# Up projections with one 512-column product for the high weights, a VectorE sum of two banks, and the gate product on GpSimd

## The chip, the cores and the metric

The kernel runs on one core of a Trainium2 chip. The core has TensorE (matmuls into PSUM, eight banks of 128 partitions x 512 float32), VectorE, ScalarE and GpSimd (elementwise work), and SyncE, which here only issues loads. The engines run side by side and are ordered by semaphores alone. The metric is the device time of one execution, in microseconds; lower is better.

## The reference

Four layers run over a residual stream x of 256 tokens x 1024 channels. Each layer has a mixer (sparse attention in layers 0 and 3, RWKV-7 in layer 1, S5 in layer 2) and then a conv-gated MLP, which is all that the change touches:

```
def conv_ffn(h, w_up, conv_w, conv_b, w_down):      # D = 1024, F = 2816
    u = h @ w_up                                     # (256, 1024) @ (1024, 5632)
    u = lax.conv_general_dilated(u, conv_w[:, None, :], ... feature_group_count=u.shape[-1]) + conv_b
    gate, val = jnp.split(u, 2, axis=-1)             # causal convolution over 3 tokens, per channel
    return (jax.nn.silu(gate) * val) @ w_down        # (256, 2816) @ (2816, 1024)

for i in range(DEPTH):                               # DEPTH = 4
    ...                                              # mixer
    h = rms_norm(x, norm_ffn[i])
    x = x + conv_ffn(h, ffn_w_up[i], ffn_conv_w[i], ffn_conv_b[i], ffn_w_down[i])
```

## The kernel before

Everything is kept transposed: channels on partitions, the T = 256 tokens along the free axis. A float32 product is made of three matmuls on rounded parts. A weight block is split into high (rounded on ScalarE, line 397) and low (what is left, line 405); the activations likewise, into x_high and x_low. `product` (line 420) issues high x high, high x low and low x high, 256 columns each, into the same 256 columns of PSUM (lines 422 to 424).

A *tile* is 1024 x 256 weights (1 MB), loaded by SyncE into a ring of three slots (line 697). It has two blocks of 128 output channels, b = 0 and 1. ScalarE rounds both blocks; VectorE computes the low part of block 0 and GpSimd that of block 1 (`rest_of_weights`, line 399). There are two buffers of split weights, so tile k + 2 is split while tile k + 1 is in use, and a block can be rounded once TensorE has done with the same block two tiles before (`ahead`, line 407; `wait_half`, line 359). SyncE reloads a slot once both low parts are made (`wait_slot`, line 680).

**The up stage** of a layer has 22 tiles in 11 pairs: tile 2j holds gate channels, 2j + 1 the value channels for them. Pairs 0 to 2 are written out, pairs 3 to 8 run in a hardware loop of two rounds, pairs 9 and 10 are written out again (`over_up_tiles`, line 755). A tile has 8 chunks x 2 blocks = 16 products. Before, both blocks of a tile go to the two halves of one PSUM bank, bank i mod 6, so six tiles fit. Pair 0 uses `early` activations, not yet scaled by the norm, and its banks are scaled afterwards (line 908). Tile 2 takes its chunks as VectorE finishes x_low (line 557).

What follows a tile: ScalarE forms tap 2 of the convolution from the bank (line 856), VectorE adds taps 1 and 0 (line 937, four instructions a tile, counting `taps_done` 2 per tile). For a pair ScalarE takes the silu of the gate half (line 862), VectorE multiplies gate and value (line 946, into `gated`), ScalarE rounds this to inner_high (line 841), and GpSimd computes inner_low (line 885, counting `inner_ready`).

**The down stage** follows on TensorE: four outputs m, three weight tiles g each. For m < 3 it already uses a pair: high weights times inner_high and inner_low as one 512-column matmul (line 824), low weights times inner_high (line 826), and VectorE adds the two halves of the bank (lines 662 and 664). m = 3 uses `product`. Output m and block b go to bank DOWN_BANKS[m] + b, for m = 0 banks 4 and 5.

Which bank TensorE may overwrite is planned ahead: `plan.fill` counts the fills of each bank, `freed` names the semaphore value at which a fill has been read, and `wait_free` (line 328) waits for that of the fill before. Layer 1 also prepares layer 2's mixer: `s5_turn_a` (line 2683) behind pair 9 and `s5_turn_c` (line 2690) behind pair 10 transpose parameters into banks 6 and 7. In layers 0 and 3 the last mixer outputs alternate between banks 0 and 1; line 642 adds them to x.

## Time and profile before

| | us |
|---|---|
| median of 3 runs | 1431.87 (1431.63 to 1433.32) |
| the profiled execution | 1431.35 |
| its span, first to last instruction | 1429.6 |

The profile is that of one execution. Engine names in it: PE is TensorE's matmuls, PEld its weight loads, DVE is VectorE, ACT ScalarE, POOL GpSimd, SP SyncE. L405 is line 405 of the kernel. Matmuls overlap, and their ends are modelled: distances between starts tell the pace. In layer 0 tile 0 starts at 154.61 us, tile 3 at 173.62, the down stage at 283.16. PEclk is the granted clock of TensorE, 1.00 being 2.4 GHz and 0.50 being 1.2 GHz.

### The profile page before, as it was taken

What the parts mean: (1) busy time and instruction counts of PE and PEld (TensorE: products, weight loads), DVE (VectorE), ACT (ScalarE), POOL (GpSimd) and SP (SyncE); (2) the same over time, 40 slices, a digit from 0 to 9 for tenths busy, and PEclk for the clock granted to TensorE, in tenths of its full rate; (3) what the DMA queues carried; (4) which work ended last, traced back from release to release, by engine and by line L of the source; (5) the groups of instructions that cost most, each with busy time, mean ns of one, the idle gap of its engine ahead of it and who ended that gap; (6) DMA issues with size and microseconds to landing.
All of it is one profiled execution on the core that took longest, in us unless ns stands there. A gap on an engine that the chain in (4) does not pass through costs nothing.

```text
span 1429.6 us, 33183 instructions
## 1 busy us (share of the span) xinstructions
PE 1378.5 (96%) x13785; PEld 1302.5 (91%) x13785; DVE 1011.5 (71%) x1604; ACT 804.3 (56%) x1331; POOL 659.0 (46%) x370
## 2 busy tenths in 40 slices
PE   8999999999999887999999889999999999999998
PEld 8999999989888777999988779999989998999988
DVE  6675887834595556897789966888746685888841
ACT  5576666644751453666554445656645577676642
POOL 4343365552003630495557945365544332365552
PEclk9999999999999999999999999999999999999999
DMA  6542455553534011475554024465554543455553
GB/s 200 183 133 96 159 196 185 184 189 119 148 124 142 4 34 32 148 224 190 169 180 153 2 62 152 148 203 178 183 197 128 179 146 119 148 179 188 186 172 102
DMA packets 208168, 209.60 MB, mean 147 GB/s; under 512 B 7954, under 2 KB 207170, under 8 KB 208034
## 3 DMA queue, kind: packets, MB, share of 16 engines
q1 hardware_dynamic: 207168, 206.21, 44.8%
q0 software_dynamic: 800, 1.46, 0.6%
q8 instruction: 100, 1.64, 0.5%
q14 instruction: 34, 0.28, 0.1%
q10 hardware_dynamic: 66, 0.02, 0.0%
HBM read 206.62 MB, written 1.05 MB: 145 GB/s over the span
## 4 chain that ended last, share of the span: by engine, by line
PE 82%; DVE 11%; ACT 4%; issue 2%; POOL 1%; DMA 0%; ACTq 0%; DVEq 0%; POOLq 0%
PE psum L422 17%; PE psum L424 17%; PE psum L423 17%; PE psum L824 9%; PE psum L605 6%; PE psum L826 4%; DVE x_low L557 2%; DVE work L2958 1%; ACT w_high L397 1%; DVE work L542 1%; PE psum L1800 1%; PE psum L1817 1%; DVE w_low L405 1%; PE psum L1089 1%; PE psum L1100 1%
## 5 line engine op out<-in xcount | busy, mean ns | idle before, releaser
L405 POOL TENSOR_TENSOR w_low<-ring,w_high 128x1024 fp32r<-128x1024 f32 (+1 forms) x185 | 460.4, 2489 | 611.4 <-ACT w_high L397 589.5
L422 PE MATMUL psum<-x_high,w_high 128*128 128x256 f32 x1728 | 491.2, 284 | 5.0 <-DVE x_low L2375 2.8
L397 ACT ACTIVATE w_high<-ring 128x1024 fp32r<-128x1024 f32 (+1 forms) x368 | 376.4, 1036 | 212.2 <-PE psum L424 119.5
L424 PE MATMUL psum<-x_high,w_low 128*128 128x256 f32 x1728 | 488.9, 283 | 0.0
L423 PE MATMUL psum<-x_low,w_high 128*128 128x256 f32 x1728 | 488.9, 283 | 0.0
L405 DVE TENSOR_TENSOR w_low<-ring,w_high 128x1024 fp32r<-128x1024 f32 x183 | 299.4, 1637 | 169.6 <-ACT w_high L397 168.2
L422 PEld LDWEIGHTS psum<-x_high,w_high 128*128 128x128 f32 x1728 | 331.6, 192 | 7.4 <-issue 3.4
L423 PEld LDWEIGHTS psum<-x_low,w_high 128*128 128x128 f32 x1728 | 331.7, 192 | 0.0
L424 PEld LDWEIGHTS psum<-x_high,w_low 128*128 128x128 f32 x1728 | 331.6, 192 | 0.0
L824 PE MATMUL psum<-inner,w_high 128*128 128x512 f32 x528 | 186.8, 399 | 0.0
L937 DVE SCALAR_TENSOR_TENSOR work<-psum,par,work 128x255 f32<-128x255 f32 (+1 forms) x352 | 144.6, 472 | 45.8 <-ACT work L856 45.7
L856 ACT ACTIVATE work<-psum,par 128x256 f32<-128x256 f32 x176 | 89.3, 561 | 131.3 <-PE psum L424 131.3
L826 PE MATMUL psum<-inner,w_low 128*128 128x256 f32 x528 | 148.3, 281 | 0.0
L824 PEld LDWEIGHTS psum<-inner,w_high 128*128 128x128 f32 x528 | 99.2, 188 | 24.6
L826 PEld LDWEIGHTS psum<-inner,w_low 128*128 128x128 f32 x528 | 99.8, 189 | 0.0
L946 DVE TENSOR_TENSOR work<-work 128x512 f32<-128x512 f32 x44 | 80.9, 1839 | 7.4 <-DVE work L937 5.5
L605 PE MATMUL psum<-work,ring 128*128 128x256 f32 x384 | 84.4, 379 | 0.9 <-issue 0.9
L605 PEld LDWEIGHTS psum<-work,ring 128*128 128x128 f32 x384 | 72.8, 190 | 13.0 <-issue 3.4
L422 PE MATMUL psum<-w_high,x_high 128*128 128x256 f32 x256 | 75.1, 293 | 0.0
L885 POOL TENSOR_TENSOR inner<-work,inner 128x512 f32 (+1 forms) x44 | 74.8, 1703 | 0.0
L424 PE MATMUL psum<-w_high,x_low 128*128 128x256 f32 x256 | 72.4, 283 | 0.0
L423 PE MATMUL psum<-w_low,x_high 128*128 128x256 f32 x256 | 72.4, 283 | 0.0
(353 smaller groups left out, 2212.0 us busy)
## 6 DMA issues: line engine op xcount, KB each, us to landing
ring<-in_ffn_w_up_dram SPq DMA_DIRECT2D x88, 1024.0 KB, 5.1
ring<-in_ffn_w_down_dram SPq DMA_DIRECT2D x32, 1024.0 KB, 5.2
ring<-in_dsa_w_in_dram SPq DMA_DIRECT2D x28, 1024.0 KB, 5.3
ring<-in_ffn_w_down_dram SPq DMA_DIRECT2D x16, 768.0 KB, 4.4
ring<-in_rwkv_w_rkv_dram SPq DMA_DIRECT2D x12, 1024.0 KB, 5.1
ring<-in_dsa_w_out_dram SPq DMA_DIRECT2D x8, 1024.0 KB, 5.4
ring<-in_s_w_glu_dram SPq DMA_DIRECT2D x8, 1024.0 KB, 5.4
ring<-in_rwkv_w_out_dram SPq DMA_DIRECT2D x4, 1024.0 KB, 5.1
```

The source lines that it names most:

```text
L397: act.activation(high, raw, ACT.Copy).then_inc(sem("w_rounded", b), 1)
L405: eng.tensor_tensor(low, raw, high.bitcast(F32), ALU.subtract).then_inc(sem("w_split", b), 1)
L422: pe.matmul(out_, lhs[0], rhs[0], start=start, stop=False, skip_group_check=True)
L423: pe.matmul(out_, lhs[0], rhs[1], start=False, stop=False, skip_group_check=True)
L424: return pe.matmul(out_, lhs[1], rhs[0], start=False, stop=stop, skip_group_check=True)
L605: mm = pe.matmul(out_, parts[b][:, k, b * P:(b + 1) * P], x[:, k, :], start=start, stop=stop, skip_group_check=True)
L824: pe.matmul(banks[bank][:, :], high[:, k, :], inner[:, :, c, :], start=first, stop=False, skip_group_check=True)
L826: mm = pe.matmul(banks[bank][:, 0:T], low[:, k, :], inner_high[:, c, :], start=False, stop=last, skip_group_check=True)
L856: act.activation(conv[:, j % 3, h, b, :], bank_of(key)[:, b * T:(b + 1) * T], ACT.Identity, bias=col("ffn_conv_b", c + L * 2 * FC, r), sca ...
L885: pool.tensor_tensor(inner_low[:, at(2 * j, r), :], gated[:, j % 3], inner_high[:, at(2 * j, r), :].bitcast(F32), ALU.subtract).then_inc(s ...
L937: dve.scalar_tensor_tensor(out=row, in0=bank[:, b * T:(b + 1) * T - lag], scalar=col("ffn_conv_w", c + (L * 3 + tap) * 2 * FC, r), in1=row ...
L946: dve.tensor_tensor(gated[:, j % 3], conv[:, j % 3, 0], conv[:, j % 3, 1], ALU.mult).then_inc(sem("gated_done"), 1)
```

## The change

From tile 2 on, the three matmuls of a product become two: high weights times x_high and x_low side by side (`x_both`, the same memory as x_high and x_low), 512 columns, which fill a whole bank, and low weights times x_high into its first half. So each block of a tile gets a bank of its own: tile i uses banks 2 (i mod 3) and the next, and three tiles fit instead of six. Tiles 0 and 1 keep the three matmuls, but use two banks too.

When a tile's two banks are full, VectorE adds their halves (`tensor_reduce` over 2 x 256 x 2 elements) into a sum bank: 6 or 7 in turn, 2 or 3 for tiles 20 and 21. Taps read the sum bank. ScalarE rounds both blocks of the tile after next before tap 2, which waits for the sum (`halves_added`). The product of gate and value moves from VectorE to GpSimd. `freed` says when a tile's banks may be filled again: after its sum for tiles 2 to 18, after its own taps for tiles 0 and 1, and after all taps of the layer (2 * FC = 44) for tiles 19 to 21. `s5_turn_a` waits for the taps of tile 18, as bank 6 is in use now.

```diff
-        simple([(L, "up", i) for i in range(2 * FC // 2)], split=True)
+        for i in range(FC):
+            plan.weights((L, "up", i), split=True)
+            for b in range(2):
+                plan.fill((L, "up", i, b), 2 * (i % (NBANK // 2)) + b)
+            plan.used[(L, "up", i)] = ("bank_full", plan.bank[(L, "up", i, 1)])
...
-                freed[(L, "up", 2 * j)] = (("taps_done", L), 4 * j + 2)
-                freed[(L, "up", 2 * j + 1)] = (("taps_done", L), 4 * j + 4)
+                for b in range(2):
+                    for h in range(2):
+                        i = 2 * j + h
+                        freed[(L, "up", i, b)] = ((("halves_added", L), i + 1) if 1 < i < FC - 3 else
+                                                  (("taps_done", L), 2 * i + 2 if i < 2 else 2 * FC))
...
+                        if j == 0:
+                            mm = product(pe, banks[bank][:, 0:T], (high, low), (early[0][:, c, :], early[1][:, c, :]),
+                                         c == 0, c == DC - 1)
+                        else:
+                            pe.matmul(banks[bank][:, :], high, x_both[:, :, c, :], start=c == 0, stop=False,
+                                      skip_group_check=True)
+                            mm = pe.matmul(banks[bank][:, 0:T], low, x_high[:, c, :], start=False, stop=c == DC - 1,
+                                           skip_group_check=True)
+                        if c == DC - 1:
+                            mm.then_inc(sem("bank_full", bank), 1)
...
+        def half_sums(key):
+            i = key[2]
+            if i < 2:
+                first = plan.bank[(*key, 0)][0]
+                return psum[:, first:first + 2, 0:T]
+            return banks[6 + i % 2 if i < FC - 2 else 2 + i % 2].rearrange("p (b t) -> p b t", b=2)
+        def halves(key):
+            first = plan.bank[(*key, 0)][0]
+            return psum[:, first:first + 2, :].rearrange("p b (a t) -> p b t a", a=2)
...
                     if j:
-                        ahead(round_weights, act, key, 0, r=r)
-                        wait_full(act, key, r)
-                    else:
-                        act.wait_ge(sem("scaled"), h + 1 + since("scaled", L))
+                        ahead(round_weights, act, key, r=r)
+                    act.wait_ge(sem("halves_added"), r * ROUND + (2 * j + h + 1 + since("halves_added", L)))
...
+            def gate_times_value(j, r):
+                pool.wait_ge(sem("silu_done"), r * PJ + (j + 1 + since("silu_done", L)))
+                pool.wait_ge(sem("taps_done"), r * (4 * PJ) + (4 * j + 4 + since("taps_done", L)))
+                if j >= 3:
+                    pool.wait_ge(sem("inner_ready"), r * PJ + (j - 2 + since("inner_ready", L)))
+                pool.tensor_tensor(gated[:, j % 3], conv[:, j % 3, 0], conv[:, j % 3, 1],
+                                   ALU.mult).then_inc(sem("gated_done"), 1)
             def pair(j, r):
+                ahead(rest_of_weights, pool, (L, "up", 2 * j), 1, r=r)
+                if j:
+                    gate_times_value(j - 1, r)
+                ahead(rest_of_weights, pool, (L, "up", 2 * j + 1), 1, r=r)
                 if j:
                     rest_of_inner(j - 1, r)
...
                 for h in range(2):
+                    key = (L, "up", 2 * j + h)
+                    sums = half_sums(key)
                     if j:
-                        ahead(rest_of_weights, dve, (L, "up", 2 * j + h), 0, r=r)
+                        both_full(key, r)
+                        dve.tensor_reduce(out=sums, in_=halves(key), op=ALU.add, axis=AX_X).then_inc(sem("halves_added"), 1)
+                        ahead(rest_of_weights, dve, key, 0, r=r)
...
-        def s5_turn_a(pe):
+        def s5_turn_a(pe, L):
             pe.wait_ge(sem("s5_in", 0), 16 * S5_DMAS[0])
+            pe.wait_ge(sem("taps_done"), 2 * (FC - 4) + 2 + since("taps_done", L - 1))
```

## Rows read from the trace of the kernel before

**Rows 1.** The page: busy time (us), share of the span and instructions per engine.

```profile
PE 1378.5 (96%) x13785; PEld 1302.5 (91%) x13785; DVE 1011.5 (71%) x1604; ACT 804.3 (56%) x1331; POOL 659.0 (46%) x370
```

**Rows 2.** The page: the chain that ended last, shares of the span by engine and by line.

```profile
PE 82%; DVE 11%; ACT 4%; issue 2%; POOL 1%; DMA 0%; ACTq 0%; DVEq 0%; POOLq 0%
PE psum L422 17%; PE psum L424 17%; PE psum L423 17%; PE psum L824 9%; PE psum L605 6%; PE psum L826 4%; DVE x_low L557 2%; DVE work L2958 1%; ACT w_high L397 1%; DVE work L542 1%; PE psum L1800 1%; PE psum L1817 1%; DVE w_low L405 1%; PE psum L1089 1%; PE psum L1100 1%
```

**Rows 3.** Busy time per stretch, layer 0's up stage and start of its down stage.

```profile
core 0: us, PE busy (x) PEld busy (x) DVE busy (x) ACT busy (x) POOL busy (x), PEclk, DMA share, GB/s
172.00:283.00 111.00, 110.71 (x923) 110.51 (x922) 92.03 (x116) 70.98 (x102) 65.51 (x29) 1.00 0.54 178
283.00:325.00 42.00, 42.00 (x240) 36.46 (x239) 16.66 (x18) 18.05 (x21) 21.38 (x10) 1.00 0.61 193
```

**Rows 4.** Timeline of PE: start us, duration us, engine, line, operation [idle before, releaser].

```profile
173.62 0.39 PE L422 MATMUL psum<-x_high,w_high 128*128 128x256 f32 x1 [0.29 <-DVE w_low L405]
...
283.16 0.40 PE L824 MATMUL psum<-inner,w_high 128*128 128x512 f32 x1
...
329.80 0.28 PE L422 MATMUL psum<-inner,w_high 128*128 128x256 f32 x1
```

**Rows 5.** Groups by form (count, busy us, mean ns, idle before); a timeline row; the page's load.

```profile
L2958 DVE TENSOR_TENSOR work<-b_sum,psum 128x1024 f32<-128x1024 f32 x4 | 4.9, 1221 | 0.1
...
791.10 2.34 DVE L2958 TENSOR_TENSOR work<-work,psum 128x1024 f32<-128x1024 f32 x2
...
L1348 DVE TENSOR_REDUCE work<-work 128x8 f32<-128x512 f32 x8 | 5.4, 680 | 0.0
L2146 POOL TENSOR_TENSOR work<-work,blocks 128x512 f32<-128x512 f32 x8 | 10.0, 1275 | 38.7 <-ACT work L2056 38.7
ring<-in_ffn_w_up_dram SPq DMA_DIRECT2D x88, 1024.0 KB, 5.1
```

**Rows 6.** Groups of instructions in the stretch 172 to 283 us.

```profile
L405 DVE TENSOR_TENSOR w_low<-ring,w_high 128x1024 fp32r<-128x1024 f32 x21 | 41.1, 1957 | 6.5 <-ACT w_high L397 6.5
L937 DVE SCALAR_TENSOR_TENSOR work<-psum,par,work 128x255 f32<-128x255 f32 (+1 forms) x84 | 34.5, 472 | 10.4 <-ACT work L856 10.4
```

**Rows 7.** Timelines of VectorE, GpSimd and ScalarE near layer 0's last up tiles.

```profile
274.64 2.23 DVE L946 TENSOR_TENSOR work<-work 128x512 f32<-128x512 f32 x1
276.79 2.31 DVE L405 TENSOR_TENSOR w_low<-ring,w_high 128x1024 fp32r<-128x1024 f32 x1
...
284.42 1.65 DVE L937 SCALAR_TENSOR_TENSOR work<-psum,par,work 128x255 f32<-128x255 f32 x4 [1.24 <-ACT work L856]
...
273.88 2.44 POOL L405 TENSOR_TENSOR w_low<-ring,w_high 128x1024 fp32r<-128x1024 f32 x1 [3.31 <-ACT w_high L397]
276.29 1.74 POOL L885 TENSOR_TENSOR inner<-work,inner 128x512 fp32r<-128x512 f32 x1
285.41 2.43 POOL L405 TENSOR_TENSOR w_low<-ring,w_high 128x1024 fp32r<-128x1024 f32 x1 [3.32 <-ACT w_high L397]
...
283.36 1.02 ACT L856 ACTIVATE work<-psum,par 128x256 f32<-128x256 f32 x2 [1.76 <-PE psum L424]
284.27 1.06 ACT L397 ACTIVATE w_high<-ring 128x1024 fp32r<-128x1024 f32 x1
```

**Rows 8.** Timeline of VectorE at layer 0's first up tiles.

```profile
172.35 1.21 DVE L405 TENSOR_TENSOR w_low<-ring,w_high 128x1024 fp32r<-128x1024 f32 x1
173.61 3.21 DVE L937 SCALAR_TENSOR_TENSOR work<-psum,par,work 128x255 f32<-128x255 f32 x8
```

**Rows 9.** Timelines of VectorE and PE around layer 0's tile 0.

```profile
154.81 0.69 DVE L642 TENSOR_TENSOR xT<-xT,psum 128x512 f32<-128x512 f32 x1 [0.92 <-PE psum L424]
...
154.61 0.28 PE L422 MATMUL psum<-early_high,w_high 128*128 128x256 f32 x1
157.84 1.10 PE L505 MATMUL psum<-work,mean_all 128*128 128x256 f32 x4 [0.19 <-DVE work L493]
```

**Rows 10.** Timeline of PE at the end of layer 1's up stage.

```profile
715.73 1.03 PE L2696 MATMUL psum<-ident,work 128*128 128x128 f32 x8
716.52 0.48 PE L824 MATMUL psum<-inner,w_high 128*128 128x512 f32 x1
```

**Rows 11.** Timeline of PE behind idle time, and the stretches around (columns as rows 3).

```profile
898.89 0.39 PE L422 MATMUL psum<-early_high,w_high 128*128 128x256 f32 x1 [1.91 <-DVE work L3068]
...
900.30 0.41 PE L422 MATMUL psum<-early_high,w_high 128*128 128x256 f32 x1
900.94 0.41 PE L422 MATMUL psum<-early_high,w_high 128*128 128x256 f32 x1
...
898.00:900.00 2.00, 1.11 (x8) 1.11 (x9) 1.53 (x3) 1.76 (x3) 0.00 (x0) 0.94 1.05 361
900.00:902.00 2.00, 2.00 (x11) 2.00 (x10) 1.54 (x3) 2.00 (x5) 0.00 (x0) 0.50 0.28 98
902.00:904.00 2.00, 2.00 (x11) 1.94 (x11) 1.23 (x1) 0.92 (x1) 1.00 (x1) 0.71 0.00 0
...
825.66 2.06 PE L2741 MATMUL psum<-work 128*64 128x32 f32 x64 [2.07 <-DVE psum L2999]
```

More of the change, by code:

```diff
@@ L54 @@
 NBANK = 6
+UP_FILLS = 2
 DOWN_BANKS = (4, 0, 2, 4)
@@ L128, in weights @@
             self.split_tiles.append(key)
-            if key[1:2] + key[3:] != ("down", 2):
+            if key[1] != "up" and key[1:2] + key[3:] != ("down", 2):
                 self.half[key] = len(self.half) + 1
@@ L783, in pair @@
                     if j >= PJ:
-                        name, value = freed[(L, "up", 2 * j + h - ROUND)]
+                        name, value = freed[(L, "up", 2 * j + h - NBANK // 2, 0)]
                         done, offset = signal(name)
-                        pe.wait_ge(done, r * (4 * PJ) + (value + offset))
+                        pe.wait_ge(done, r * ROUND + (value + offset))
                     else:
-                        wait_free(pe, key)
-                    bank = plan.bank[key][0]
+                        for b in range(2):
+                            wait_free(pe, (*key, b))
                     parts, first = {}, h == 0 and j < 2
-                    high, low = early if j == 0 else (x_high, x_low)
                     for c, b in chunks_and_blocks(DC, first):
@@ L797, in pair @@
                             parts[b] = split_weights(pe, key, b, r)
-                        mm = product(pe, banks[bank][:, b * T:(b + 1) * T], (parts[b][0][:, c, :], parts[b][1][:, c, :]),
-                                     (high[:, c, :], low[:, c, :]), c == 0 and (b == 0 or not first), c == DC - 1)
-                        half_done(key, mm, b == 0 and c == DC - 1)
-                    mm.then_inc(sem("bank_full", bank), 1)
+                        high, low, bank = parts[b][0][:, c, :], parts[b][1][:, c, :], plan.bank[(*key, b)][0]
+                        if j == 0:
[8 more added lines that the diff above has]
+                            mm.then_inc(sem("bank_full", bank), 1)
                 if before_s5(L) and j == UP_TILES // 2 - 2:
-                    s5_turn_a(pe)
+                    s5_turn_a(pe, L + 1)
                 if before_s5(L) and j == UP_TILES // 2 - 1:
@@ L896, in mlp_pool @@
             over_up_tiles(pool, pair)
+            gate_times_value(UP_TILES // 2 - 1, 0)
             rest_of_inner(UP_TILES // 2 - 1, 0)
@@ L937, in pair, with both_full @@
                             dve.scalar_tensor_tensor(
-                                out=row, in0=bank[:, b * T:(b + 1) * T - lag],
+                                out=row, in0=sums[:, b, 0:T - lag],
                                 scalar=col("ffn_conv_w", c + (L * 3 + tap) * 2 * FC, r),
                                 in1=row, op0=ALU.mult, op1=ALU.add).then_inc(done, 1)
-                dve.wait_ge(sem("silu_done"), r * PJ + (j + 1 + since("silu_done", L)))
-                dve.wait_ge(sem("taps_done"), r * (4 * PJ) + (4 * j + 4 + since("taps_done", L)))
-                if j >= 3:
-                    dve.wait_ge(sem("inner_ready"), r * PJ + (j - 2 + since("inner_ready", L)))
-                dve.tensor_tensor(gated[:, j % 3], conv[:, j % 3, 0], conv[:, j % 3, 1],
-                                  ALU.mult).then_inc(sem("gated_done"), 1)
+            def both_full(key, r):
+                for b in range(2):
+                    bank, n = plan.bank[(*key, b)]
+                    dve.wait_ge(sem("bank_full", bank), r * UP_FILLS + n)
             over_up_tiles(dve, pair)
```

27 lines of the change are left out of this document (14 added, 13 removed).

## The prediction

> **What bounds the kernel now.** I read the page's totals first: TensorE is busy 96% of the span, VectorE 71%, GpSimd 46% [rows 1]. The chain that ended last agrees: 82% of it is TensorE, led by the three product lines 422 to 424 [rows 2]. The busy time per stretch then shows how full the up stage of layer 0 is: from 172 to 283 us TensorE is busy 110.7 of 111 us, and in the down stage that follows 42.0 of 42 [rows 3]. So both stages run at the pitch of the matmuls, and any wait put on TensorE is paid in full. A matmul's printed duration (0.28 or 0.40 us) is not its price, because neighbours overlap; the start-to-start distance is.
>
> **What the pair saves.** The up stage issues triples of 256 columns. From the first matmul of tile 3 at 173.62 to the first of the down stage at 283.16 are 19 tiles of 16 triples: 109.54 / 304 = 0.3603 us each. The down stage already issues the pair that the change introduces (512 columns, then 256): from 283.16 to 329.80 are 132 pairs, 0.3533 us each [rows 4]. The 512-column matmul takes the time of the two it replaces, and only 0.007 us per triple is left. Tiles 3 to 21 save 304 x 0.0070 = 2.13 us per layer, 8.5 us in four. Tile 2 saves nothing: it follows x_low, which VectorE finishes late. A tile becomes 16 x 0.3533 = 5.65 us long.
>
> **What it costs in steady state.** Per tile VectorE loses half a gate product and gains a reduce over 1024 PSUM elements. The nearest rows are VectorE operations on 1024 elements with a PSUM operand, 1.22 us, or 1.13 start to start; TENSOR_REDUCE itself is seen only at 512 elements, 0.68 us as other operations of that size [rows 5]. I take 1.14; twice that is the upper end, as this reduce writes 512 results and reads across two banks.
>
> The real price is in how VectorE and GpSimd meet. The split of a weight block takes VectorE 1.21 us alone [rows 8], but 1.96 on average in the up stage, while its taps stay at 0.47 [rows 6]. The timeline shows why. The gate product asked at 274.64 while GpSimd's split ran 273.88 to 276.32, and ended at 276.87: 0.55 after. VectorE's split asked at 276.79 while GpSimd's L885 ran until 278.03, and ended at 279.10: 1.07 after [rows 7]. An operation of one with two SBUF inputs waits until the other's is done. The order is by who asks first, and a waiting VectorE gets its turn between two GpSimd operations: L885 takes 1.74 here, where GpSimd alone takes 1.28 for that size [rows 5]. The Trainium skill (SBUF — State Buffer, "SBUF: two separate sides") calls it an exclusive lock, held for the whole instruction by whoever starts first. By that rule the forecast below holds; were it a shared rate, VectorE would finish earlier and the time be nearer my first rival.
>
> The change lets ScalarE round block 1 before tap 2. The last tile shows the clock of this: TensorE's next matmul starts at 283.16, ScalarE notices the full bank at 283.36 [rows 4, 7]. Rounding takes 1.06 and GpSimd starts 0.08 later (285.41 behind 284.27 + 1.06): here at 284.50. VectorE reduces from 283.36 to 284.50 at best, and then asks for its own split. It is a tie; but each time GpSimd wins, VectorE's split ends 2.43 + 1.07 later, at 288.00, and its four taps (0.05 + 1.65) at 289.70; 0.08 on, who waits for them goes on. That is 6.6 us after the tile's end, 0.95 more than a tile lasts. So VectorE begins the next reduce 0.95 late, GpSimd, which follows TensorE and ScalarE, wins surely, and the state keeps itself. I take it. TensorE isn't held: the split is ready 4.9 us into a tile of 5.65, and banks come free by the reduce with two tiles to spare. SyncE's next load waits for that split and lands 5.1 us later [rows 5], about 10 us after the tile's end, where ScalarE wants it at 2.5 tiles, 14.1.
>
> The new waits hold little up. ScalarE's tap 2 waits for the reduce until about 2.1 us into the tile; behind it stands the rounding of the next block, wanted from 2.8. GpSimd's gate product waits for taps that end 0.95 us into the tile, before its first split there; behind it stand a split with a tile to spare and the rest of inner. With 2 x 2.43 + 2 x 1.28 = 7.4 of 11.3 us per pair [rows 5, 6] GpSimd has room. In the late state even a reduce of 2.3 us hides, since it ends before GpSimd's split does.
>
> **What it costs at the ends.** Banks are the point: a tile now takes two, so only three tiles fit.
> - *Down stage.* Its first product fills banks 4 and 5, last used by tile 20, and freed[...] of tile 20 is `taps_done` at 2 * FC: every tap of tile 21 too. Before, it waited for tile 16, long done. So TensorE stands from the end of tile 21 to the end of its taps, with all down products queued behind: 289.78 - 283.16 = 6.6 us in the late state, 4.3 if VectorE wins the lock (reduce to 284.5, split to 285.7, taps to 287.4). I take 6.6: four layers, 26.4 us. The chain behind it hides: gate product on GpSimd, rounding and rest of inner end at about 293.1, and TensorE needs the last of them 32 pairs (11.3 us) after 289.8.
> - *Tile 3.* It reuses banks 0 and 1 and waits for tile 0's taps, instead of only for its own weights. VectorE starts them at 173.61, eight in 3.21 us, so the first four end at 175.3 [rows 8]: 1.73 us later than the start at 173.62, 6.9 in four layers. Tiles 4 and 5 find their banks free.
> - *Tile 0 in layers 0 and 3.* Bank 1 makes it wait for the last residual addition, which ends at 155.50; TensorE had started it at 154.61. With 24 matmuls before the mean, this comes at 158.45 instead of 157.84 [rows 9]. The VectorE chain behind (root, x_low, scale, taps) shifts by 0.6: 1.2 us in two layers.
> - *Layer 1.* `s5_turn_a` now waits for tile 18's taps, 6.6 - 5.65 = 1.0 us in the late state; `s5_turn_c`, 0.8 us on TensorE's path before (715.73 to 716.52), falls into the stall [rows 10]. Net 0.1.
>
> **The clock.** TensorE's granted clock is 1.0 (2.4 GHz) nearly everywhere. After 1.91 us of idle before 898.89 it falls to 0.50 (1.2 GHz) at about 899.8 and is back by 904; matmuls then start 0.21 us apart instead of 0.12. The shares of rows 898 to 904 add up to 3.4 us at half clock, 1.7 us lost. After 2.07 us of idle at 825.66 no fall follows at once [rows 11]. No row shows 6.6 us of idle. The cost lies between 0 and 1.7 us a stall; part of the low stretch may lie in the idle itself, so I take 1.3: 5.2 us. The Trainium skill (TensorE: Matmul & The Clock Gate, "Why this matters for your kernels") says that an idle gap of this kind returns the array to half clock; by it the term is near its upper end, without it nothing, 1457.4 us in all.
>
> **The sum**, against the profiled execution (1431.35 us, span 1429.6; the median of the runs is 1431.87, 0.5 more): 1431.35 - 8.5 + 26.4 + 6.9 + 1.2 + 0.1 + 5.2 = 1462.6 us, 2.2% slower.
>
> **Rivals.**
> - *VectorE wins the lock.* If its reduce ends before ScalarE's rounding does, there is no lag: each end stall is 4.3, not 6.6, and the wait of `s5_turn_a` goes. 1462.6 - 9.2 - 1.0 = 1452.4. For it: 0.1 us decides. Against it: once lost, it stays lost.
> - *No clock fall* in either state: 5.2 less, 1457.4 or 1447.2. For it: the idle at 825.66. The reverse, a fall after the 2.2 us stall at tile 3 as well, adds up to 6.8: 1469.
> - *GpSimd keeps the lock* for its gate product too. VectorE's split ends 1.28 later, at 6.1 of 5.65 us, TensorE waits 0.56 at every second tile, 9 x 4 times: +20, 1483. Against it: VectorE got its turn both times in [rows 7]. A reduce above some 2.8 us would end as badly, at 0.1 us x 76 tiles for each tenth more.
> - *Faster.* The pair runs quicker than in the down stage. At half clock 256 columns start 0.213 us apart (three steps from 900.30 to 900.94 [rows 11]), one column a cycle of 1.2 GHz; 768 columns at 2.4 GHz would be 0.320 us, my estimate; 1216 pairs at that pitch give 40.5 more, 1422.1. It decides from 0.3533 - 31.3 / 1216 = 0.3276 us. Against it: 132 pairs of the same form at 0.3533 [rows 4].
>
> **How the numbers follow.** Forecast 0.52 (its own range 1457 to 1469, with or without the clock's fall and one more). VectorE wins 0.30 (1447 to 1454). GpSimd keeps the lock or the reduce is the bound 0.11 (above 1470). Quicker pair 0.04, and 0.03 for something unseen that cancels half of the stalls. For 8 in 10: 1447 to 1471. A measurement can tell 0.2%, 2.9 us, from no change. Faster 0.04, the same 0.01, slower 0.95.
>
> **What would show it.** In the changed profile: pairs 0.353 us apart in the up stage; TensorE idle 6 to 7 us before the first product of each down stage, released by VectorE's taps; about 1.7 to 2.3 us before tile 3, with the same releaser; the reduce at 1.1 to 1.3 us; VectorE's split at some 3 us on average; the granted clock near 0.5 behind the stalls. Wrong if TensorE goes from tile 21 into the down stage without a gap, if the pitch is under 0.33, or if the idle of TensorE is spread over the tiles.

## The result and the profile after

| | before | after |
|---|---|---|
| median, us | 1431.75 (4 runs, 1431.16 to 1433.32) | 1467.27 (4 runs, 1461.57 to 1477.06) |
| ratio to before, 95% interval | | 1.0247 [1.0216, 1.0278] |
| profiled execution, us | 1431.35 | 1464.49 (span 1462.8) |

The changed kernel is 2.5% slower. The profiled execution, at +33.1 us, is one of the faster ones of the four.

The page of after, busy time per engine, and the chain that ended last, by engine:

```profile
PE 1373.0 (94%) x12505; PEld 1237.6 (85%) x12505; DVE 1079.7 (74%) x1640; ACT 811.9 (56%) x1331; POOL 743.0 (51%) x414
...
PE 55%; DVE 29%; issue 10%; ACT 4%; POOL 1%; DVEq 1%; DMA 0%; ACTq 0%; POOLq 0%
```

Beside [rows 1, 2]: TensorE has 1280 matmuls fewer and yet only 5.5 us less busy time. Its share of the chain falls from 82% to 55%, and VectorE's grows from 11% to 29%. The kernel now waits for VectorE somewhere. The page doesn't say where; the timeline does. These are rows of PE in after, columns as in [rows 4]. Line 813 is the new 512-column product, 815 the 256-column one behind it, 841 the first product of the down stage (824 before), 982 the taps (937 before), 416 the low parts (405 before):

```profile
176.11 0.47 PE L813 MATMUL psum<-x_both,w_high 128*128 128x512 f32 x1 [2.14 <-DVE work L982]
...
187.28 0.39 PE L813 MATMUL psum<-x_both,w_high 128*128 128x512 f32 x1
...
192.83 0.39 PE L813 MATMUL psum<-x_both,w_high 128*128 128x512 f32 x1
...
281.46 0.28 PE L815 MATMUL psum<-x_both,w_low 128*128 128x256 f32 x1
288.01 0.77 PE L841 MATMUL psum<-inner,w_high 128*128 128x512 f32 x1 [6.27 <-POOL inner L911]
...
640.12 0.50 PE L813 MATMUL psum<-x_both,w_high 128*128 128x512 f32 x1 [1.88 <-DVE w_low L416]
...
1288.92 0.40 PE L813 MATMUL psum<-x_both,w_high 128*128 128x512 f32 x1
...
1294.58 0.40 PE L813 MATMUL psum<-x_both,w_high 128*128 128x512 f32 x1
```

Tile 3 waits 2.14 us for the taps of tile 0. Tiles 5 and 6 of layer 0 start 187.28 and 192.83, so one pair of matmuls (512 columns, then 256) takes 5.55 / 16 = 0.347 us there; in layer 3 it is 5.66 / 16 = 0.354. The down stage begins 6.4 us after the last up product. In layer 1 a gap stands in the middle of the stage.

VectorE, ScalarE and GpSimd at the end of layer 0's up stage in after (968 is the new reduce, 408 the rounding of a block, 911 inner_low):

```profile
282.37 1.22 DVE L968 TENSOR_REDUCE psum<-psum 128x512 f32<-128x1024 f32 x1
283.50 2.84 DVE L416 TENSOR_TENSOR w_low<-ring,w_high 128x1024 fp32r<-128x1024 f32 x1
286.26 1.64 DVE L982 SCALAR_TENSOR_TENSOR work<-psum,par,work 128x255 f32<-128x255 f32 x4
...
281.78 1.06 ACT L408 ACTIVATE w_high<-ring 128x1024 fp32r<-128x1024 f32 x1 [1.65 <-PE psum L815]
...
282.91 2.35 POOL L416 TENSOR_TENSOR w_low<-ring,w_high 128x1024 fp32r<-128x1024 f32 x1 [0.88 <-ACT w_high L408]
```

This is the late state that the prediction took. VectorE begins the reduce at 282.37, later than it could (ScalarE had noticed the full bank at 281.78). GpSimd's low part starts at 282.91, ahead of VectorE's at 283.50, which ends at 286.34, 1.08 behind GpSimd's 285.26. The four taps end at 287.90, and TensorE goes on 0.11 later: 6.43 us after the tile's end, counted from the start of its last matmul plus the 0.12 us that one such matmul takes in the stream. Gaps in the table below are counted this way; the number in brackets in a row is the idle time by the profile, a little less. The profile writes L911 as the releaser, but the end of the taps fits as well, and the edit in the first experiment, which concerns the taps alone, removes the gap.

The late state doesn't begin with the stage. Behind tiles 2 and 3 of layer 0 VectorE still asks first (178.62 against 179.15, and 183.15 against 183.35). Behind tile 4 GpSimd is ahead by 0.07 us, and from there on VectorE stays late. VectorE and GpSimd in after:

```profile
188.69 3.44 DVE L416 TENSOR_TENSOR w_low<-ring,w_high 128x1024 fp32r<-128x1024 f32 x1
...
188.62 2.43 POOL L416 TENSOR_TENSOR w_low<-ring,w_high 128x1024 fp32r<-128x1024 f32 x1 [0.59 <-ACT w_high L408]
```

Groups of instructions of after from 180 to 280 us (as [rows 6]); 921 is the gate product on GpSimd:

```profile
L416 DVE TENSOR_TENSOR w_low<-ring,w_high 128x1024 fp32r<-128x1024 f32 x18 | 51.6, 2864 | 0.0
...
L968 DVE TENSOR_REDUCE psum<-psum 128x512 f32<-128x1024 f32 x18 | 22.0, 1220 | 1.9 <-PE psum L815 1.9
...
L921 POOL TENSOR_TENSOR work<-work 128x512 f32<-128x512 f32 x10 | 21.8, 2181 | 0.0
```

Busy time per stretch of after around the stall, columns as in [rows 3]:

```profile
282.00:284.00 2.00, 0.00 (x0) 0.00 (x0) 2.00 (x4) 1.21 (x2) 1.12 (x2) 1.00 0.93 293
284.00:286.00 2.00, 0.00 (x0) 0.00 (x0) 2.00 (x1) 1.68 (x4) 1.50 (x2) 0.55 0.65 230
286.00:288.00 2.00, 0.00 (x0) 0.03 (x1) 1.91 (x5) 0.00 (x0) 1.47 (x1) 0.50 0.20 50
288.00:290.00 2.00, 1.99 (x6) 1.71 (x7) 0.00 (x0) 0.63 (x1) 1.27 (x1) 0.50 0.99 347
290.00:292.00 2.00, 2.00 (x11) 1.75 (x10) 0.00 (x0) 0.00 (x0) 1.28 (x1) 0.74 0.36 128
```

TensorE's granted clock goes from 1.00 (2.4 GHz) to 0.50 (1.2 GHz) while TensorE stands idle. The shares of these stretches (1.8 + 2.0 + 2.0 + 1.0) make 6.8 us at half clock, about 3 us of it behind the restart. In layer 2 it is the same, but in layers 1 and 3 the low stretch starts only 1.2 to 1.3 us before the restart, and 5.5 us of it lie behind. Layer 1, where TensorE restarts at 732.60:

```profile
736.00:738.00 2.00, 2.00 (x8) 1.71 (x8) 0.00 (x0) 0.00 (x0) 0.00 (x0) 0.50 0.00 0
```

Where the 33.1 us are, from the same places of both traces:

| term | predicted | measured |
|---|---|---|
| pairs in tiles 3 to 21 | -8.5 | -14.3 (-4.07 in layers 0, 1, 2; -2.13 in layer 3) |
| last up to first down product | +26.4 | +25.7 (6.43, 6.42, 6.43, 6.42) |
| before tile 3 | +6.9 | +6.7 (tile 2 to 3: 6.21, 6.31, 6.30, 6.29 became 7.95, 7.96, 7.95, 7.97) |
| tile 0, mixers, tile 1 | +1.2 | +2.4 (0.75 of it at tile 0 of layer 0) |
| layer 1, `s5_turn_a`, `s5_turn_c` | +0.1 | +0.1 (0.85 of new idle, 0.79 of `s5_turn_c` now hidden) |
| layer 1, TensorE waits for VectorE's split | 0 | +3.1 (2.03 at 640.12, 1.10 at 646.88) |
| clock: down stages, behind tile 3 of layer 3 | +5.2 | +9.0 (1.4, 1.9, 1.4, 2.6, and 1.7) |
| sum | +31.3 | +32.7 |

0.4 us stay unassigned; they lie in layer 1.

### The profile page after: what moved, and what is told of

It reads as the page before. It is cut to its first block, busy times and chain, and to the rows that moved or that the text cites. A ratio compares the mean times of both kernels' runs of the same rounds, so it can differ in the third digit from the quotient of the medians.

```text
span 1462.8 us, 30758 instructions
## 1 busy us (share of the span) xinstructions
PE 1373.0 (94%) x12505; PEld 1237.6 (85%) x12505; DVE 1079.7 (74%) x1640; ACT 811.9 (56%) x1331; POOL 743.0 (51%) x414
## 4 chain that ended last, share of the span: by engine, by line
PE 55%; DVE 29%; issue 10%; ACT 4%; POOL 1%; DVEq 1%; DMA 0%; ACTq 0%; POOLq 0%
DVE w_low L416 9%; PE psum L841 9%; PE psum L433 7%; PE psum L435 7%; PE psum L434 7%; PE psum L616 5%; DVE psum L968 5%; DVE work L982 5%; PE psum L843 4%; PE psum L813 3%; ACT w_high L408 2%; DVE x_both L568 2%; PE psum L815 1%; DVE work L3001 1%; DVE work L553 1%
## 5 line engine op out<-in xcount | busy, mean ns | idle before, releaser
L416 DVE TENSOR_TENSOR w_low<-ring,w_high 128x1024 fp32r<-128x1024 f32 x183 | 361.7, 1978 | 172.4 <-ACT w_high L408 171.4
L813 PE MATMUL psum<-x_both,w_high 128*128 128x512 f32 x1280 | 449.0, 396 | 11.4 <-DVE work L982 8.6
L815 PE MATMUL psum<-x_both,w_low 128*128 128x256 f32 x1280 | 358.3, 280 | 0.0
L813 PEld LDWEIGHTS psum<-x_both,w_high 128*128 128x128 f32 x1280 | 240.7, 188 | 68.8 <-DVE work L982 9.7
L815 PEld LDWEIGHTS psum<-x_both,w_low 128*128 128x128 f32 x1280 | 242.2, 189 | 0.0
L841 PE MATMUL psum<-inner,w_high 128*128 128x512 f32 x528 | 193.6, 410 | 24.2 <-POOL inner L911 24.2
L841 PEld LDWEIGHTS psum<-inner,w_high 128*128 128x128 f32 x528 | 103.0, 195 | 50.7 <-POOL inner L911 25.3
L433 PE MATMUL psum<-x_both,w_high 128*128 128x256 f32 x448 | 128.6, 287 | 2.3 <-DVE x_both L2417 1.6
L435 PE MATMUL psum<-x_both,w_low 128*128 128x256 f32 x448 | 126.7, 283 | 0.0
L434 PE MATMUL psum<-x_both,w_high 128*128 128x256 f32 x448 | 126.7, 283 | 0.0
L968 DVE TENSOR_REDUCE psum<-psum 128x512 f32<-128x1024 f32 x80 | 97.6, 1220 | 8.2 <-PE psum L815 8.2
L921 POOL TENSOR_TENSOR work<-work 128x512 f32<-128x512 f32 x44 | 91.4, 2078 | 2.3 <-issue 2.3
L433 PEld LDWEIGHTS psum<-x_both,w_high 128*128 128x128 f32 x448 | 85.9, 192 | 3.9 <-DVE x_both L2417 1.8
L434 PEld LDWEIGHTS psum<-x_both,w_high 128*128 128x128 f32 x448 | 86.0, 192 | 0.0
L435 PEld LDWEIGHTS psum<-x_both,w_low 128*128 128x128 f32 x448 | 85.9, 192 | 0.0
```

Source lines behind the costliest of these rows:

```text
L416: eng.tensor_tensor(low, raw, high.bitcast(F32), ALU.subtract).then_inc(sem("w_split", b), 1)
L433: pe.matmul(out_, lhs[0], rhs[0], start=start, stop=False, skip_group_check=True)
L434: pe.matmul(out_, lhs[0], rhs[1], start=False, stop=False, skip_group_check=True)
L435: return pe.matmul(out_, lhs[1], rhs[0], start=False, stop=stop, skip_group_check=True)
L813: pe.matmul(banks[bank][:, :], high, x_both[:, :, c, :], start=c == 0, stop=False, skip_group_check=True)
L815: mm = pe.matmul(banks[bank][:, 0:T], low, x_high[:, c, :], start=False, stop=c == DC - 1, skip_group_check=True)
```

## The experiments

### The wait at the down stage, taken away: e1_end

In the changed kernel, the banks of tiles 20 and 21 count as free after the tile's own sum (tile 19's can't, since sums go into its banks).

```diff
-  freed[(L, "up", i, b)] = ((("halves_added", L), i + 1) if 1 < i < FC - 3 else
+  freed[(L, "up", i, b)] = ((("halves_added", L), i + 1) if 1 < i and i != FC - 3 else
```

> The changed kernel (1464.5 us in its profiled run) with one edit: tiles 20 and 21 free their banks after their own sums, as tiles 2 to 18 do, instead of after all taps of the layer. My theory: the wait is 6.4 us of idle TensorE in each layer, and the fall of the clock behind it another 1.4 to 1.7; both go. Four times 7.8 to 8.1 is 31 to 32 us, so about 1433 us, with no gap before the first product of a down stage and no low clock there. Rival: another wait takes its place, because the gate product, its rounding and the rest of inner end too late for the third weight tile of the first output. Then TensorE stands 1 to 4 us before that tile instead, and the time is 1437 to 1449. A side question is the pace of the pair, 0.3466 us in most up stages of the changed kernel and 0.3533 in the down stages. If the pace is set by how a stream of matmuls starts and then lasts, the down stage now inherits 0.3466 and gains 0.85 us a layer; if it belongs to the operand (inner against x_both), the down stage stays at 0.3533.

Measured: median 1439.05 (6 runs), ratio 1.0032 [1.0013, 1.0051], 28.2 us under after by the medians. Beside these runs, and those of the next three experiments, the kernel before took 1433.38 us and not 1431.75; by the two ratios to before the gain is 2.15%, 30.8 us. The gap is gone in all four layers. The timeline of PE in e1_end, the end of layer 0's up stage:

```profile
285.76 0.28 PE L815 MATMUL psum<-x_both,w_low 128*128 128x256 f32 x1
285.88 0.40 PE L841 MATMUL psum<-inner,w_high 128*128 128x512 f32 x1
```

So one semaphore value in the plan carried most of the loss; what made the wait that long was how late VectorE ran (see e3_order). By the ratios the gain is what was expected, by the medians some 3 us short of it. The median lies in the range of the rival, but the rival's gap before the third weight tile isn't there (layer 0's down products take as long as in the kernel before, 46.29 us from the first to the last pair). The profiled run (1442.64, the slowest of the six) shows one thing that can make the runs differ: the clock fell behind the 2.1 us gap at tile 3 in three of four layers, where in after it fell in one. The stretches of e1_end behind it in layer 0:

```profile
178.00:180.00 2.00, 2.00 (x8) 1.71 (x7) 2.00 (x3) 2.00 (x3) 0.08 (x1) 0.50 0.66 157
```

### The wait at tile 3, taken away: e2_start

Tiles 0 and 1 get a sum bank as well: VectorE scales them from banks 0 to 3 into bank 6 or 7 at once, and their banks count as free then (`halves_added`).

```diff
-  freed[(L, "up", i, b)] = ((("halves_added", L), i + 1) if 1 < i < FC - 3 else
+  freed[(L, "up", i, b)] = ((("halves_added", L), i + 1) if 0 <= i < FC - 3 else
...
-            if i < 2:
-                first = plan.bank[(*key, 0)][0]
-                return psum[:, first:first + 2, 0:T]
...
-  dve.tensor_tensor(sums, sums, rstd[:, :]...
+  first = plan.bank[(L, "up", h, 0)][0]
+  dve.tensor_tensor(sums, psum[:, first:first + 2, 0:T], rstd[:, :]...
```

> The changed kernel with one edit: the sums of tiles 0 and 1 are written into banks 6 and 7, so that their own banks are free once they are scaled, and tile 3 needn't wait for tile 0's taps. My theory: the idle of 2.14 us before tile 3 shrinks to the 0.3 us that the kernel before has there, 1.8 us in each layer, and the fall of the clock that follows it in some layers (1.7 us in layer 3 of the profiled run) can't come: 7 to 9 us faster than the changed kernel, about 1456 us. Rival on the pace of the pair: if the faster 0.3466 us exists only because the stream starts behind a gap, the up pairs now run at 0.3533, cost 2.0 us more in each layer that ran fast, and the edit gains next to nothing, 1462 to 1465. If the pace belongs to the operand, it stays at 0.3466.

Measured: 1460.01 (4 runs), ratio 1.0185 [1.0168, 1.0202], 7.3 us under after, within the 7 to 9 expected (8.9 by the ratios; the expected 1456 was counted from the profiled run of after, which is quicker than its median). In the timeline of PE the tile now waits 0.49 us, for its weights as in [rows 4]:

```profile
174.75 0.47 PE L813 MATMUL psum<-x_both,w_high 128*128 128x512 f32 x1 [0.49 <-DVE w_low L416]
```

The pairs still run at 0.347 us in three of four layers (here 0, 2 and 3), so the gap before tile 3 isn't what makes them quicker than predicted.

### ScalarE's old order: e3_order

ScalarE rounds block 1 behind tap 2 again, so that GpSimd's split asks about 1 us later than VectorE's.

```diff
-                        ahead(round_weights, act, key, r=r)
+                        ahead(round_weights, act, key, 0, r=r)
...
+                    if j:
+                        ahead(round_weights, act, key, 1, r=r)
```

> The changed kernel with one edit: ScalarE rounds block 1 of the tile after next behind tap 2 again, as the kernel before does, so GpSimd asks for its split some 2 us later and VectorE, which asks behind its reduce, comes first. My theory (one operation with two SBUF inputs at a time, first asked first served): VectorE's split falls from 2.9 us to about 1.25, its taps end 4.2 us behind the last tile instead of 6.4, and the time falls by 2.2 us in each layer, plus up to 1 us in layer 1, to 1454 to 1456. Rival: VectorE's lateness comes from the reduce or from the number of its instructions, not from who asks first. Then its split stays at 2.5 us or more and the time within 2 us of the changed kernel.

Measured: 1456.78 (4 runs), ratio 1.0165 [1.0145, 1.0185], 10.5 us under after. Groups of e3_order from 180 to 280 us, and the rows of VectorE and PE at the end of layer 0's up stage:

```profile
L416 DVE TENSOR_TENSOR w_low<-ring,w_high 128x1024 fp32r<-128x1024 f32 x18 | 26.9, 1497 | 0.0
...
283.06 1.37 DVE L416 TENSOR_TENSOR w_low<-ring,w_high 128x1024 fp32r<-128x1024 f32 x1
...
286.09 0.77 PE L841 MATMUL psum<-inner,w_high 128*128 128x512 f32 x1 [4.28 <-issue]
```

VectorE's split fell from 2864 to 1497 ns, the end gaps from 6.4 to 4.4 us (4.44, 4.35, 4.43, 4.34; in layer 1 that includes 0.8 us of `s5_turn_c`), and layer 1's gaps are gone. The rival "VectorE wins the lock" is thus real, and priced at 4.3 us a stall as worked out; the change's own order decides against it. What doesn't go is a stall of 4.4: VectorE's reduce, split and taps still stand between the last tile and the down stage.

### The wait alone, in the kernel before: e4_before_wait

The kernel before, with one wait added ahead of the down stage's first product. Nothing else is changed: triples, six banks, gate product on VectorE.

```diff
+                        if g == 0 and m == 0:
+                            pe.wait_ge(sem("taps_done"), 2 * FC + since("taps_done", L))
```

> The kernel before with one wait added: the first product of each down stage waits for all taps of the layer. It prices the wait without the rest of the change. In its trace the taps of the last tile end at 286.06 where TensorE would go on at 283.16, so 3.0 us of idle in each layer, 12 us in four. If the granted clock falls behind such a gap each time, 1.4 to 1.7 us more each: 1449 to 1451. If it falls only behind longer ones: 1443 to 1445. If the pace of the pair is set by how the stream starts, a down stage that starts behind a gap and sees no fall runs at 0.3466 us instead of 0.3533, 0.9 us less a layer (1440); if not, it stays at 0.3533.

Measured: 1447.5 (4 runs), ratio 1.0094 [1.0077, 1.0111], 14.1 us over the kernel before (1433.38), between the two times that were expected. From the last up product to the first down product it is 3.16 us in layers 0, 2 and 3; here the taps are named as the releaser. In layer 1 it is 3.16 too, but `s5_turn_c`, 0.79 us on TensorE's path before as well, fills part of it, so the wait adds 2.37 there: 11.8 us together. PE in e4_before_wait in layers 0 and 1, and its stretches behind the gap of layer 1 and behind that of layer 3:

```profile
286.06 0.47 PE L826 MATMUL psum<-inner,w_high 128*128 128x512 f32 x1 [3.00 <-DVE work L939]
...
720.97 1.03 PE L2698 MATMUL psum<-ident,work 128*128 128x128 f32 x8
724.13 0.47 PE L826 MATMUL psum<-inner,w_high 128*128 128x512 f32 x1 [2.13 <-DVE work L939]
...
724.00:728.00 4.00, 3.87 (x22) 3.42 (x23) 2.17 (x1) 1.56 (x3) 4.00 (x3) 1.00 0.34 109
...
1380.00:1384.00 4.00, 4.00 (x17) 3.43 (x16) 0.68 (x1) 0.84 (x1) 1.29 (x2) 0.67 0.72 251
```

Behind 3.0 us of idle the clock fell, in layers 0, 2 and 3; behind 2.13 us, in layer 1, it stayed, and 22 matmuls start in 4 us against 17. The wait costs its gap and 2.3 us more over the four layers. In the profiled execution (1450.05, the slowest of the four) the clock takes time in three layers, and two down stages give some back: the pair takes 0.347 us in those of layers 0 and 1, 0.353 in those of layers 2 and 3.

### Both waits away: e5_both

The edits of e1_end and e2_start together.

> The changed kernel with both waits on TensorE eased together: the banks of tiles 20 and 21 come free after their own sums (as in e1_end), and the sums of tiles 0 and 1 lie in banks 6 and 7 (as in e2_start). Theory: the two gains add up. The first edit alone gave 1439.1 against 1467.3, 28 us; the second alone 7.3. Together about 1432, and 2 to 4 less because without the 2.3 us gap at tile 3 the clock doesn't fall there (it fell in three of four layers in the profiled run of e1_end): 1428 to 1431, so at or just under the kernel before. Rival: the two share one cause (a late VectorE), and the second edit only shifts the wait to the next tile; then 1436 to 1439.

Measured: 1428.79 (5 runs), ratio 0.9965 [0.9952, 0.9978]. The effects add up: in ratio to before, 0.0215 and 0.0062 alone, 0.0282 together. Rid of the two waits the change is 0.35% faster than before, so the pair, the reduce and the moved gate product together are a small gain, and the loss was in when banks come free.

### ScalarE's order on top: e8_both_order

e5_both with the edit of e3_order.

> As e5_both, and ScalarE rounds block 1 behind tap 2 (as in e3_order). Theory: with the end wait gone VectorE's lateness costs nothing except in layer 1, where e1_end shows 1.5, 1.8 and 1.1 us of idle TensorE (VectorE's split held up by GpSimd, and the wait for tile 18's taps); so 3 to 5 us under e5_both, 1424 to 1427. Rival: GpSimd's later split holds TensorE up at block 1, or the rest of inner comes too late for the down stage: slower than e5_both by 2 us or more.

Measured: 1432.2 (12 runs), ratio 0.9991 [0.9981, 1.0000]. Missed: 3.4 us slower than e5_both instead of quicker. PE, and VectorE and GpSimd, in layer 1 of e8_both_order (920 is the gate product, 910 inner_low there):

```profile
628.39 0.50 PE L813 MATMUL psum<-x_both,w_high 128*128 128x512 f32 x1 [0.93 <-POOL w_low L416]
...
625.93 7.11 DVE L416 TENSOR_TENSOR w_low<-ring,w_high 128x1024 fp32r<-128x1024 f32 x1
...
625.93 2.40 POOL L416 TENSOR_TENSOR w_low<-ring,w_high 128x1024 fp32r<-128x1024 f32 x1
628.30 1.27 POOL L920 TENSOR_TENSOR work<-work 128x512 f32<-128x512 f32 x1
629.54 2.41 POOL L416 TENSOR_TENSOR w_low<-ring,w_high 128x1024 fp32r<-128x1024 f32 x1
631.92 2.26 POOL L910 TENSOR_TENSOR inner<-work,inner 128x512 fp32r<-128x512 f32 x1
```

Both splits start at 625.93 by the profile, and GpSimd wins. It then runs three operations back to back at their undisturbed lengths; only the fourth is stretched (2.26 instead of 1.28), and that is where VectorE's 1.2 us fit. TensorE waits 1.8 us for VectorE's split, at 633.09. The prediction's "a waiting VectorE gets its turn between two GpSimd operations" is not a rule. What starts it is likely local: GpSimd also issues 14 S5 parameter loads in this layer, four of them from 622.86 to 625.93 right ahead of these rows, and then has a queue of operations ready. No run without these loads was made.

This isn't the whole of the 3.4 us. e5_both has such holds too, two in layer 1 (VectorE's split takes 5.25 and 5.37 us, TensorE idles 0.91 and 1.06). Against them e8_both_order has idles of 0.93 us, released by GpSimd's split as in the row of PE above, which is the first half of the rival, of 1.66, and of 1.00 at 745.42 in the down stage: 1.6 us more. The rest stays unexplained; the two profiled executions lie only 0.5 us apart.

### Other banks in layers 0 and 3: e6_banks

e8_both_order, with tiles starting at bank 2 in layers 0 and 3, away from the mixer's output in banks 0 and 1.

```diff
-  plan.fill((L, "up", i, b), 2 * (i % (NBANK // 2)) + b)
+  plan.fill((L, "up", i, b), 2 * ((i + (kind == 0)) % (NBANK // 2)) + b)
```

The sums of tiles 20 and 21 stay in banks 6 and 7 in those layers, and every tile's banks are free after its sum.

> As e8_both_order, and in layers 0 and 3 the tiles start at banks 2 and 3 instead of 0 and 1, so that tile 0 needn't wait for the last residual addition. Theory: the 1.0 us gap before tile 0 in these two layers goes, and tile 3 comes 0.6 to 0.75 us earlier in each: 1.2 to 1.5 us under e8_both_order. Rival: the start of tile 3 is set by VectorE's chain that begins with the same residual addition, not by the mean; then no difference.

Measured: 1429.86 (12 runs), ratio 0.9983 [0.9971, 0.9995]; 2.3 us under e8_both_order by the medians, in intervals that overlap, so the gain isn't certain. The gap of 0.99 us before tile 0 is gone in layers 0 and 3, which is the part the trace shows.

### The gate product back on VectorE: e7_gate_vector

e8_both_order, with `gate_times_value` in VectorE's order, where it was before.

```diff
-                if j:
-                    gate_times_value(j - 1, r)
...
+                dve.tensor_tensor(gated[:, j % 3], conv[:, j % 3, 0], conv[:, j % 3, 1],
+                                  ALU.mult).then_inc(sem("gated_done"), 1)
```

> As e8_both_order, but the product of gate and value is back on VectorE: it isolates that part of the change. Theory: VectorE then has about 2 x (1.13 + 1.21 + 1.65) + 0.6 = 8.6 us of its own work in 11.1 us per pair and waits for GpSimd's two splits at most once each; TensorE is held at no tile, and the time is within 2 us of e8_both_order. So moving the gate product bought nothing. Rival: with the waits for GpSimd VectorE becomes the bound, as the change assumes; then TensorE waits for its splits in each pair, 1 us or more x 9 x 4, and the time is above 1455.

Measured: 1425.69 (7 runs), ratio 0.9952 [0.9935, 0.9969], 6.5 us under e8_both_order, more than the 2 us that were allowed for. Groups of e7_gate_vector from 180 to 280 us (955 is the reduce, 978 the gate product):

```profile
L416 DVE TENSOR_TENSOR w_low<-ring,w_high 128x1024 fp32r<-128x1024 f32 x19 | 23.6, 1242 | 0.0
...
L978 DVE TENSOR_TENSOR work<-work 128x512 f32<-128x512 f32 x9 | 18.2, 2021 | 1.4 <-DVE work L969 1.1
...
L955 DVE TENSOR_REDUCE psum<-psum 128x512 f32<-128x1024 f32 x18 | 22.1, 1226 | 6.1 <-PE psum L815 6.1
```

VectorE carries reduce and gate product and still waits 6.1 of 100 us for TensorE; its split takes 1242 ns, nearly the undisturbed 1.21 of [rows 8]. What waits for GpSimd now is the gate product: 2021 ns on average, where it takes 0.69 alone (e10_gate_late). Layer 1's gaps of 0.9 to 1.7 us are gone; the largest left in that stage, 0.5 us before tile 3, stands in the other layers too. With this order the move to GpSimd was a loss. The gaps of layer 1 were worth about 3 us; the rest of the 6.5 isn't traced.

### Both: e9_all

e7_gate_vector with the banks of e6_banks.

> The version that the runs so far point to: the 512-column pair, banks freed by the sums at both ends, ScalarE's block 1 behind tap 2, tiles of layers 0 and 3 starting at banks 2 and 3, and the gate product on VectorE. e7_gate_vector without the bank order gave 1425.7; the bank order alone took 2.3 off e8_both_order. Theory: the gains add up, 1422.5 to 1425, 0.6 to 0.7% under the kernel before. Rival: the spread of the runs is set by the pace of the pair (0.3466 or 0.3533 us, which takes or leaves up to 8 us over four up stages and 3 over the down stages) and by falls of the clock in the mixers, and hides 1.5 us; then 1425 to 1427.

Measured: 1426.95 (7 runs, 1419.94 to 1430.58), ratio 0.9957 [0.9938, 0.9976], in the range of the rival. It can't be told from e7_gate_vector: the runs of one kernel spread over more than the 1 to 2 us in question. Its profiled execution, 1420.95, has the quicker pace in three of four up stages and in all four down stages.

### The gate product back, in the change's order: e10_gate_late

e5_both with the edit of e7_gate_vector, to see whether the move to GpSimd pays where ScalarE rounds block 1 early.

> As e5_both (VectorE late behind GpSimd's split), with the gate product back on VectorE. It asks what moving that product bought in the order that the change has. Theory: nothing. VectorE's taps end 6.4 us behind the tile, the gate product 0.7 later, and the next reduce still ends before GpSimd's split (1.3 + 2.4 us into the tile) lets VectorE go on, so TensorE waits at no tile: within 2 us of e5_both (1428.8), or up to 4 us faster because layer 1 loses one of GpSimd's operations between which VectorE is passed over. Rival: VectorE falls behind by 0.7 to 2 us a pair and TensorE waits for its split of block 0: 10 pairs x 4 x 0.7 or more, above 1455.

Measured: 1442.9 (6 runs), ratio 1.0074 [1.0053, 1.0095], 14.1 us over e5_both: missed, and between the theory and the rival. The loss is one gap per layer, before tile 4 (2.69, 3.16, 2.68, 2.70), and a fall of the clock behind it in three layers (not in layer 1, the longest of the four). PE, VectorE and GpSimd in e10_gate_late (976 is the gate product of pair 0):

```profile
182.97 0.47 PE L813 MATMUL psum<-x_both,w_high 128*128 128x512 f32 x1 [2.53 <-DVE w_low L416]
...
177.87 0.69 DVE L976 TENSOR_TENSOR work<-work 128x512 f32<-128x512 f32 x1
179.61 3.21 DVE L416 TENSOR_TENSOR w_low<-ring,w_high 128x1024 fp32r<-128x1024 f32 x1
...
179.35 2.39 POOL L416 TENSOR_TENSOR w_low<-ring,w_high 128x1024 fp32r<-128x1024 f32 x1 [2.56 <-ACT w_high L408]
```

and in e5_both at the same place:

```profile
178.95 1.21 DVE L416 TENSOR_TENSOR w_low<-ring,w_high 128x1024 fp32r<-128x1024 f32 x1
...
179.49 2.97 POOL L416 TENSOR_TENSOR w_low<-ring,w_high 128x1024 fp32r<-128x1024 f32 x1 [2.57 <-ACT w_high L408]
```

0.69 us of gate product put VectorE's split 0.26 us behind GpSimd's request instead of 0.54 ahead. It then ends at 182.82 instead of 180.16, and the weights of tile 4 are wanted by 180.3. What the moved product is worth can't be told without the order around it: 14 us gained in the change's order, 6.5 lost in ScalarE's old one.

## Why the prediction was right, and where its steps were off

**The forecast, 1462.6 us, and its sign hold;** the median of 1467.27 is inside the range. The mechanisms that it named carry the result:

- *The end wait.* Predicted 6.6 us a layer, measured 6.4, with the chain of steps as written down: GpSimd's split first, VectorE's 1.08 behind it, four taps, 0.11 to the restart. e1_end shows that the freed value of tiles 20 and 21 is the cause, e4_before_wait that the same wait costs about its gap in the old kernel too, and e3_order that 2 of the 6.4 us come from who asks first.
- *The lock.* The prediction took the late state over its rival at a tie of 0.1 us; the trace shows it in every layer, and e3_order shows the other state with the predicted size. It was a tie: VectorE won behind tiles 2 and 3 of layer 0, and lost behind tile 4 by 0.07 us. That a state once lost keeps itself was right; that it was lost at all was in part luck, as the chance of 0.30 for the rival says. The exclusive lock of the Trainium skill (SBUF — State Buffer, "SBUF: two separate sides") agrees: in the rows shown the two splits never run side by side; VectorE's takes 1.21 us alone, and otherwise ends 1.08 us after GpSimd's (286.34 against 285.26).
- *Tile 3*, 6.7 of 6.9, and *the reduce*, 1220 ns of 1.1 to 1.3.
- *Tile 0:* 0.75 predicted as 0.6. The other 0.9 us of that row of the table is the sum of mixer stretches that shifted both ways (from -1.51 to +2.08); the sum had no term for them.

**The pace was mis-sized: -14.3 where the sum had -8.5.** The step took 0.3533 us from 132 pairs of one down stage. The pace isn't one number. In all traces the same pair of instructions runs at 0.347 or at 0.353 to 0.354 us, for the whole of an unbroken stretch, and where it changes there is a stop, be it a short one: in e6_banks layer 0 goes from 0.347 to 0.353 at an idle of 0.27 us (at 291.93, in the down stage). In e1_end, where nothing breaks the stream between the stages, each of the down stages followed closely (layers 0, 2, 3) runs at the pace of the up stage ahead of it; in e4_before_wait, where a gap does, down stages of layers 0 and 1 run at 0.347 and those of 2 and 3 at 0.353. In before the down stage ran directly behind triples and showed only the slower. What selects the pace stays open; e2_start excludes that it takes the gap at tile 3. The rival "faster" (0.320) was the right question with too large a size.

**The clock was mis-sized: +9.0 where the sum had +5.2.** The step took 1.3 of 1.7 us per end stall, with 3.4 us at half clock as its upper end, and no fall at tile 3. The half-clock stretch at a 6.4 us stall is 6.8 us long, and 3.0, 5.6, 3.1 and 5.5 us of it lie behind the restart; half of that, 1.5, 2.8, 1.5 and 2.8, is lost. The table has 1.9 for layer 1, because that down stage also ran at the quicker pace, 0.9 us less. Layer 3 had the fall at tile 3 that stood among the rivals. The Trainium skill (TensorE: Matmul & The Clock Gate, "Why this matters for your kernels") says that idling returns the array to half clock: so it was behind 8 of 8 of the long stalls (after and e2_start, 5.4 to 6.3 us of idle), but not behind every shorter one. By idle time it was 3 of 3 at 4.2 to 4.3 us and 0 of 1 at 3.3 (e3_order), 3 of 3 at 3.0 and 0 of 1 at 2.1 (e4_before_wait), and 3 of 3 at 2.5 and 0 of 1 at 3.0 (e10_gate_late).

**One step was false: "a waiting VectorE gets its turn".** It rested on two meetings in [rows 7]. It held in the steady state of layers 0, 2 and 3, and failed in layer 1, where VectorE's split took 5.63 us, with three operations of GpSimd ahead of it. VectorE and GpSimd in layer 1 of after:

```profile
634.44 5.63 DVE L416 TENSOR_TENSOR w_low<-ring,w_high 128x1024 fp32r<-128x1024 f32 x1
...
634.09 1.28 POOL L921 TENSOR_TENSOR work<-work 128x512 f32<-128x512 f32 x1
635.34 2.41 POOL L416 TENSOR_TENSOR w_low<-ring,w_high 128x1024 fp32r<-128x1024 f32 x1
637.72 1.26 POOL L911 TENSOR_TENSOR inner<-work,inner 128x512 fp32r<-128x512 f32 x1
```

This is the rival "GpSimd keeps the lock", priced at +20 for all layers; it came in one, at +3.1. That GpSimd's queue has other work in layer 1 could have been read from before. The price itself had a slip: a split ready at 6.1 us in a tile of 5.65 holds TensorE up by 0.45 us, not 0.56, which makes +16.

**That it came within 2 us of the profiled run was luck, as errors of both signs met:** -5.8 from the pace against +3.8 from the clock, +3.1 from the lock in layer 1 and +1.2 from mixers. The stalls, 32.4 of 33.1 us, were the sure part. The median lies 2.8 us over the profiled run: the runs of after spread over 15.5 us, those of before over 2.2. Which stretch gets which pace and which gaps a fall follows are two things that differ between profiles and could make this spread; it wasn't separated.

## What to carry to other kernels

Before counting matmuls saved, count who frees the PSUM banks that the wider product needs: the saving was 14 us here and one conservative semaphore value (all taps of the layer, where the tile's own sum was enough) cost 28 to 31. When two engines share a lock, plan who asks first and keep the slower one's queue from running ahead: a shift of 0.7 to 1 us in one request changed results by 10 and 14 us (e3_order, e10_gate_late), and by 3 us the other way once the waits were gone (e8_both_order). The best version measured, with e9_all beside it, keeps the wide product, frees banks by the sum, rounds block 1 behind tap 2 and leaves the gate product on VectorE: 0.9952 [0.9935, 0.9969] of before.

## What the runs showed of the hardware that was not expected

- The pair of 512 and 256 columns has two paces, 0.347 and 0.353 us, each kept through hundreds of pairs, across stages, and changed only at a stop (0.27 us is enough in e6_banks).
- A waiting VectorE can be behind three GpSimd operations in a row (7.11 us for an operation of 1.21, e8_both_order), and elsewhere gets in after one.
- Whether the clock falls behind a gap doesn't go by its length alone. Behind the equal gaps at tile 3, 2.1 us of idle each, it fell in 1 of 4 layers (after), 3 of 4 (e1_end) and 1 of 4 (e3_order). The same 1.91 us of idle stand before tile 0 of layer 2 in all twelve profiles, and the clock fell behind it in eight. In e10_gate_late it fell behind 2.5 us three times and not behind 3.0. Behind 5.4 to 6.3 us it fell each time.
